# Low weight parts of 19 projection units per layer built by an adding transfer instead of a VectorE subtraction

## The chip, the core and the metric

The kernel runs on one core of a Trainium2 chip. The metric is the device time of one execution in microseconds (us); lower is better. A core has five engines that run their own instruction streams and meet only at semaphores: TensorE (PE, matrix products into PSUM), VectorE (DVE), ScalarE (ACT), GpSimd (POOL) and SyncE (SP), which here only issues transfers. POOL can issue transfers too.

## The reference

Two sequences of 256 tokens, width 1024, go through the same two layers. All numbers are fp32.

```python
def hybrid_layer(h, w_in, ..., ln2_g, ln2_b):
    proj = h @ w_in
    q, k, v, z, xbc, dt_raw = split(proj)
    q, k = rope(q), rope(k)
    attn_out = window_attention(q, k, v, attn_sink)      # 8 heads, 2 key heads, window 128
    xs, bm, cm = split(silu(depthwise_conv(xbc, 5 taps)))
    y = bidir_ssd(xs, dt_raw, ..., bm, cm) + ssd_d * xs  # 16 heads, two directions, chunks of 128
    ssd_out = rms_norm(y * silu(z), ssd_norm_g)
    mix = concatenate([attn_out, ssd_out]) @ w_out
    h = layer_norm(ALPHA * h + mix, ln1_g, ln1_b)
    gate, val = split(h @ w_up, 2)
    ffn = (silu(depthwise_conv(gate, 3 taps)) * val) @ w_down
    return layer_norm(ALPHA * h + ffn, ln2_g, ln2_b)
```

A layer norm stands in front of the first layer.

## The kernel before, in words

**Units.** All weights of a layer are cut into 105 units of 128 x 1024 fp32 (512 KB): unit 0 is the dt projection, 1 to 6 the keys, values and queries, 7 to 18 the channels of the convolution (`U_CONV` = 7), 19 to 26 the gate z (`U_Z` = 19), 27 to 38 the output projection (`U_OUT` = 27), 39 to 82 the up projection, 83 to 104 the down projection. Each lies in a slot of a ring of five (`RING` = 5, `AHEAD` = 4), in three tiles: `raw` as loaded by SP (line 477), `whi`, its value rounded to fp32r, and `wlo` = raw - whi. Activations are split in the same way (`hhi`, `hlo`), and each product of fp32 matrices is three products: hi x hi, lo x hi, hi x lo.

The three products in `three`:

```python
843    mm(out, whi[:, slot, cols], xhi, start=start, stop=False)
844    mm(out, whi[:, slot, cols], xlo, start=False, stop=False)
845    return mm(out, wlo[:, slot, cols], xhi, start=False, stop=stop)
```

**How a unit gets ready.** SP loads it once PE has used the unit five before it (`unit_used`). ACT copies it into `whi` (line 595) and raises `unit_hi`. DVE subtracts (line 1285) and raises `unit_split`, for which PE waits before it uses the unit. ACT and DVE do these at places of the schedule: step S (n) is both, SH (n) is ACT alone and SL (n) DVE alone.

**The order of work.** `mixer_schedule` writes a list of steps by hand, once; the programs of PE, ACT, DVE and POOL all walk through it and each does its own part of a step and skips the rest. The loop is over n = 0 to 26, a projection unit G (n) on PE in each round (24 products of 128 x 512), with other work between: in rounds 8 to 15 one pair i = n - 8 of the attention (a block of 128 queries with four heads): AS (scores, PE, line 1207), AM (mask and maximum, DVE), AX (exponentials, ACT), AD (denominators, DVE, line 1615), AN (scores times 1/denominator, POOL, line 556), and, a round later, AP (8 transposes on PE, line 1217: the first four wait for the first half of AN, the others for the second) and PT (ACT copies these to SBUF, line 782); AV (probabilities times values, PE, line 1227) comes after every second pair. ACT's part of a round of the attention is, in order, PT (i-1), AX (i), SH (n+4); POOL's is AN (i) and, from round 11 on, XS (line 564) and MV (line 575). Rounds 7 to 18 also carry the convolution: ACT centre tap (line 693), DVE four taps (line 1448), ACT tanh (SILU, line 728), DVE product (SIL2, line 1455), PE transposes T (line 1132), ACT evacuation (line 746).

From round 17 on come eight pairs of the state space part: SB and SF (PE, lines 1166 and 1177) give logarithms of decays in PSUM, SC (DVE, line 1559, two instructions) caps them, SE (ACT, lines 759 and 765) takes exponentials, SW (DVE, lines 1564 and 1568) adds and multiplies, SO (DVE, line 1574) multiplies the pair's `e_off`, SD (PE, line 1193, 32 small products) uses both, SY and SG (DVE) gather the result. After round 26 the output projection begins (GA, then G with `by_rows`, lines 980 to 982), while DVE and ACT finish the root mean square.

**The entry.** DVE normalises the four blocks of tokens (lines 1342 and 1345), PE transposes them (line 972 for the later ones), POOL makes `hlo` of the first sequence (line 531), then runs three memsets (lines 546 to 548) which the mixer's steps AA and SM need, then goes into the schedule. POOL's four loads of parameters (lines 542 and 543, two a layer) are the only transfers that it issues.

Of the kernel before, what the change touches and what calls it, by code (L numbers as in the profile page):

```python
# [19 lines left out]
ALU = mybir.AluOpType  # L20
ACT = mybir.ActivationFunctionType
# [4 lines left out]
DEPTH, D_MODEL, SEQ, NSEQ = 2, 1024, 256, 2  # L26
TOK = NSEQ * SEQ
BLK = 128
NBLK = TOK // BLK
# [5 lines left out]
CT = D_MODEL // P  # L35
# [9 lines left out]
U_CONV = 7  # L45
N_CONV = 12
U_Z = U_CONV + N_CONV
U_OUT = 27
N_OUT = 12
U_UP = U_OUT + N_OUT  # L50
U_DOWN = U_UP + 2 * FT
UNITS = U_DOWN + FT
RING = 5
AHEAD = RING - 1
LAST = 3
FINAL = 4
# [35 lines left out]
def mixer_schedule():  # L92
    steps = []
    for n in range(U_OUT):
        i = n - A0
        steps += [("G", n), ("E", n)]
        if U_Z <= n < U_OUT - 1:
            steps += [("SW", n - U_Z)]
# [4 lines left out]
        if i in (3, 5, 7):  # L103
            steps += [("AV", (i - 3) // 2)]
        if U_CONV < n < U_Z - 1:
            steps += [("SL", n - 1 + AHEAD)]
# [40 lines left out]
        if U_CONV <= n < U_Z:  # L147
            steps += [("SILU", n - U_CONV)]
            if not 0 <= i < 3:
                steps += [("SIL2", n - U_CONV)]  # L150
            if n == 17:
                steps += [("MV", 2), ("MV", 3)]
            if n - U_CONV >= 4:
                steps += [("XS", n - U_CONV)]
            if n == U_Z - 1:
                steps += [("SL", n - 1 + AHEAD)]
        if 15 <= n < 17:
            steps += [("MV", n - 15)]
        if n == 17:
            steps += [("SB", 0), ("SE", 0), ("SC", 0)]  # L160
        elif a >= 0:
            if a >= 1:
                steps += [("SD", a - 1)]
            if a < 7:
                steps += [("SB", a + 1), ("SE", 3 * a + 3)]
            if a == 0:
                steps += [("SC", 1), ("SE", 4), ("SO", 0)]
            elif a < 7:
                steps += [("SO", a), ("SC", a + 1), ("SE", 3 * a + 4)]
            else:  # L170
                steps += [("SW", 7), ("SO", 7)]
            steps += [("SL", n - 1 + AHEAD)]
            if a >= 1:
                steps += [("SY", a - 1)]
# [6 lines left out]
    steps += [("GA", (U_OUT, (2, 3))), ("GA", (U_OUT, (0, 1))), ("SD", 7), ("SY", 7), ("SG", 7), ("GA", (U_OUT, (4, 5)))]  # L181
    steps += [("RP", 1), ("RP", 3)] + [("SQ", c) for c in range(4, CT)] + [("RP", 5), ("RP", 7), ("SL", U_OUT - 1 + AHEAD)]
    steps += [("GA", (U_OUT + 1, range(6))), ("GA", (U_OUT + 2, range(6))), ("RS", 0)]
# [27 lines left out]
def trunk(nc, x_in, units, pm_d, pf_d, cn_d, gb_d, h_d, y_d):  # L211
    ctx = ExitStack()
    with ctx:
# [3 lines left out]
        def sem(name):  # L217
            return ctx.enter_context(nc.semaphore(name))
# [80 lines left out]
        def f(view):  # L299
            return view.bitcast(F32)  # L300
# [44 lines left out]
        h_spilled, h_loaded, gb_loaded, affined = sem("h_spilled"), sem("h_loaded"), sem("gb_loaded"), sem("affined")  # L345
        y_scaled, y_ready = sem("y_scaled"), sem("y_ready")

        h_low, h_lows, entry_low = sem("h_low"), sem("h_lows"), sem("entry_low")
# [68 lines left out]
        def unit(L, n):  # L417

            return L * UNITS + n

        def wait_high(eng, idx, s, j):
# [102 lines left out]
        def _(pool):  # L524
# [10 lines left out]
            for L in range(DEPTH):  # L535
# [8 lines left out]
                if L == 0:  # L544
                    lows(0)
                nc.gpsimd.memset(ln_dt[:, :, :, 1, :], 0.0).then_inc(ln_zeroed, 1)
                nc.gpsimd.memset(la_sides[:, 512:528], 0.0).then_inc(ln_zeroed, 1)
                nc.gpsimd.memset(f(off_w[:]), 0.0).then_inc(off_zeroed, 1)
                pool.wait_ge(pm_loaded, L * 16 + 16)
                for what, i in SCHED:  # L550
                    if what == "AN":

# [32 lines left out]
        def _(act):  # L585
            A = nc.scalar.activation

            def split(m):

                if m < DEPTH * UNITS:  # L590
                    act.wait_ge(raw_loaded[m % RING], (m // RING) * 16 + 16)
                    if m % UNITS == U_DT:
                        A(dt_part(whi, m, 0), dt_raw(m), ACT.Copy).then_inc(unit_hi, 1)
                    else:
                        A(whi[:, m % RING, :], raw[:, m % RING, :], ACT.Copy).then_inc(unit_hi, 1)  # L595

            def squares(idx, t):
# [240 lines left out]
        def _(pe):  # L838
# [92 lines left out]
            def first_units(idx, used):  # L931

                split_units = range(idx % 2 == 0, 2)
                pe.wait_ge(unit_split, used + 1)
                for j in range(2):
                    wait_low(pe, idx, 0, j)
                    for kind in ("hi hi", "hi lo"):
                        part(idx, used, 0, 0, kind, (2 * j, 2 * j + 1))
                pe.wait_ge(unit_split, used + 2)
                for kind in ("hi hi", "hi lo"):  # L940
# [11 lines left out]
                transposes(idx, 3)  # L952
                pe.wait_ge(unit_split, used + 3)
                for kind in ("hi hi", "hi lo", "lo hi"):
# [58 lines left out]
            def final_units(units4, used):  # L1013

                for t in range(NBLK):
                    for half in range(2):
                        for j, (slot, xhi, xlo) in enumerate(units4):
                            if t == 0 and half == 0:
                                pe.wait_ge(unit_split, used + j + 1)
                            last = three_rows(2 * t + half, slot, xhi, xlo, False, j == FINAL - 1)  # L1020
                        if half or t == NBLK - 1:
                            last.then_inc(acc_done, 1)
# [16 lines left out]
            for L in range(DEPTH):  # L1039
                for what, i in SCHED:  # L1040
# [7 lines left out]
                    elif what == "G" and i < U_OUT:  # L1048
# [7 lines left out]
                        elif i - 2 >= U_Z:  # L1056
                            pe.wait_ge(zs_done, L * CT + i - 2 - U_Z + 1)
                        pe.wait_ge(unit_split, L * UNITS + i + 1)
                        by_columns(unit(L, i) % RING, unit_bank(i))
                    elif what == "G":  # L1060
                        k = i - U_OUT
                        pe.wait_ge(unit_split, L * UNITS + i + 1)
                        before = None
# [9 lines left out]
                    elif what == "GT":  # L1073
                        pe.wait_ge(unit_split, unit(L, U_UP))
                        pe.wait_ge(sl_done, L * CT + CT)
                        last_units(2 * L + 1, [(unit(L, U_OUT + k) % RING, ahi[:, k, :], alo[:, k, :])
                                               for k in range(N_OUT - LAST, N_OUT)])
                    elif what == "GA":


                        u, banks = i
                        pe.wait_ge(unit_split, L * UNITS + u + 1)
                        if u == U_OUT and 2 in banks:
# [157 lines left out]
                for k in range(1, FT):  # L1241

                    if k >= 4:
                        pe.wait_ge(glu_done, L * FT + k - 3)
                    for half in range(1 if k == 1 else 0, 2):
                        n = U_UP + 2 * k + half
                        pe.wait_ge(unit_split, unit(L, n) + 1)
                        by_columns(unit(L, n) % RING, PAIR_BANK[k % 4] + half)

                count = LAST if L < DEPTH - 1 else FINAL  # L1250
                for k in range(FT - count):
                    pe.wait_ge(unit_split, unit(L, U_DOWN + k) + 1)
                    pe.wait_ge(glu_ready, L * FT + k + 1)
# [9 lines left out]
                if L < DEPTH - 1:  # L1263
                    pe.wait_ge(unit_split, unit(L, UNITS))
                pe.wait_ge(glu_ready, L * FT + FT)
# [8 lines left out]
        def _(dve):  # L1274
            V = nc.vector

            def split(m):

                if m < DEPTH * UNITS:
                    dve.wait_ge(unit_hi, m + 1)  # L1280
# [524 lines left out]
```

## Time and profile before

| | |
|---|---|
| median of 3 runs | 1307.52 us (1306.70 to 1307.57) |
| profiled execution | 1307.72 us |
| its span | 1305.9 us |
| PE busy | 1291.5 us (99%) |
| DVE busy | 823.5 us (63%) |
| ACT busy | 580.6 us (44%) |
| POOL busy | 96.6 us (7%) |
| granted clock of PE | 0.999 of full speed |

The span runs from the first to the last instruction; the rest of the execution's time lies around it. The ends of matmuls are modelled and overlap with the next, so a busy share of PE says little: one that waits shows as a gap before an instruction, with the releaser's name in brackets. Times of instructions below are us from the span's start.

### The profile page before, as it was taken

To read this page: it belongs to the slowest core of one execution; us is meant where nothing else is said; L and a number is where in the kernel's file an instruction comes from. 1 tells how busy PE (TensorE), PEld (TensorE's weight loads), DVE (VectorE), ACT (ScalarE), POOL (GpSimd) and SP (SyncE) were. 2 spreads that over 40 slices of the span, in tenths; PEclk is the share of its full clock that TensorE was granted. 3 is DMA by queue.
4 is the path that set the end of the run, shared out by engine and by line. 5 is a ranking of instruction groups with operands and counts; after the bars stand their busy time and mean duration, and the time that the engine had idled before them with its cause. 6 is when DMAs were issued, how large, how long until landed. Compare 5 with 4: busy or idle time off the path is not lost.

```text
span 1305.9 us, 16383 instructions
## 1 busy us (share of the span) xinstructions
PE 1291.5 (99%) x6688; PEld 1066.9 (82%) x6688; DVE 823.5 (63%) x1109; ACT 580.6 (44%) x875; POOL 96.6 (7%) x87
## 2 busy tenths in 40 slices
PE   9999999999999999999999999999999999999997
PEld 8877777889888888888898777778888888888886
DVE  7888799966444444342378987999654444443425
ACT  5766655436333333311276665544453333332112
POOL 2013400001000000000020234000000000000000
PEclk9999999999999999999999999999999999999999
DMA  5422212523333333333133212143233333333332
GB/s 188 163 68 56 65 59 65 182 62 126 96 97 98 96 99 95 128 98 97 55 129 135 65 50 81 52 143 113 82 98 97 98 97 97 97 97 128 98 97 112
DMA packets 33787, 129.24 MB, mean 99 GB/s; under 512 B 3793, under 2 KB 4209, under 8 KB 32561
## 3 DMA queue, kind: packets, MB, share of 16 engines
q1 hardware_dynamic: 33552, 127.91, 30.8%
q8 instruction: 53, 0.87, 0.3%
q0 software_dynamic: 160, 0.29, 0.1%
q14 instruction: 22, 0.17, 0.0%
HBM read 121.89 MB, written 6.29 MB: 98 GB/s over the span
## 4 chain that ended last, share of the span: by engine, by line
PE 90%; DVE 7%; issue 1%; ACT 1%; DMA 0%; DVEq 0%
PE ps L843 17%; PE ps L845 16%; PE ps L844 16%; PE ps L980 9%; PE ps L982 9%; PE ps L981 9%; PE ps L869 4%; PE ps L1193 1%; PE ps L1207 1%; PE ps L1217 1%; PE ps L1227 1%; DVE e_fwd L1559 1%; PE ps L972 1%; DVE e_fwd L1564 1%; DVE e_off L1574 1%
## 5 line engine op out<-in xcount | busy, mean ns | idle before, releaser
L843 PE MATMUL ps<-hhi,whi 128*128 128x512 f32 x1040 | 409.5, 394 | 0.0
L845 PE MATMUL ps<-hhi,wlo 128*128 128x512 f32 x1040 | 405.0, 389 | 0.0
L844 PE MATMUL ps<-hlo,whi 128*128 128x512 f32 x1040 | 404.8, 389 | 0.0
L1285 DVE TENSOR_TENSOR wlo<-raw,whi 128x1024 fp32r<-128x1024 f32 x208 | 253.9, 1222 | 150.3 <-ACT whi L595 150.3
L595 ACT ACTIVATE whi<-raw 128x1024 fp32r<-128x1024 f32 x208 | 219.3, 1056 | 218.0 <-DMA raw<-in_units 218.0
L843 PEld LDWEIGHTS ps<-hhi,whi 128*128 128x128 f32 x1040 | 195.2, 188 | 44.2 <-issue 4.9
L845 PEld LDWEIGHTS ps<-hhi,wlo 128*128 128x128 f32 x1040 | 195.2, 188 | 41.4
L844 PEld LDWEIGHTS ps<-hlo,whi 128*128 128x128 f32 x1040 | 195.3, 188 | 39.4
L980 PE MATMUL ps<-whi,uhi 128*128 128x512 f32 x352 | 137.1, 390 | 0.0
L982 PE MATMUL ps<-wlo,uhi 128*128 128x512 f32 x352 | 137.0, 389 | 0.0
L981 PE MATMUL ps<-whi,ulo 128*128 128x512 f32 x352 | 136.9, 389 | 0.0
L1660 DVE SCALAR_TENSOR_TENSOR gcv<-ps,pf,gcv 128x510 f32<-128x510 f32 x44 | 32.9, 748 | 157.2 <-ACT gcv L813 157.2
L813 ACT ACTIVATE gcv<-ps,pf 128x512 f32<-128x512 f32 x44 | 34.3, 780 | 168.9 <-PE ps L845 162.1
L1670 DVE TENSOR_TENSOR guf<-gsg,ps 128x512 f32<-128x512 f32 x44 | 30.2, 687 | 79.0 <-PE ps L845 78.4
L981 PEld LDWEIGHTS ps<-whi,ulo 128*128 128x128 f32 x352 | 66.1, 188 | 13.8
L982 PEld LDWEIGHTS ps<-wlo,uhi 128*128 128x128 f32 x352 | 66.1, 188 | 13.8
L980 PEld LDWEIGHTS ps<-whi,uhi 128*128 128x128 f32 x352 | 66.1, 188 | 13.5
L1448 DVE SCALAR_TENSOR_TENSOR cv<-ps,pm,cv 128x508 f32<-128x508 f32 (+1 forms) x96 | 71.4, 744 | 7.3 <-ACT cv L693 3.0
L980 PE MATMUL ps<-whi,ahi 128*128 128x512 f32 x192 | 75.8, 395 | 0.2
L981 PE MATMUL ps<-whi,alo 128*128 128x512 f32 x192 | 74.8, 389 | 0.0
L982 PE MATMUL ps<-wlo,ahi 128*128 128x512 f32 x192 | 74.8, 389 | 0.0
L531 POOL TENSOR_TENSOR hlo<-hfm,hhi 128x512 fp32r<-128x512 f32 x16 | 21.9, 1378 | 638.1 <-ACT hhi L630 637.8
(182 smaller groups left out, 1488.2 us busy)
## 6 DMA issues: line engine op xcount, KB each, us to landing
raw<-in_units SPq DMA_DIRECT2D x208, 512.0 KB, 3.7
gb<-in_gb SPq DMA_DIRECT2D x5, 1024.0 KB, 5.8
h_kept<-hb SPq DMA_DIRECT2D x2, 2048.0 KB, 9.2
ha<-h_kept SPq DMA_DIRECT2D x2, 2048.0 KB, 8.0
hb<-in_x SPq DMA_DIRECT2D x4, 512.0 KB, 5.9
out_y<-hb SPq DMA_DIRECT2D x8, 256.0 KB, 2.0
cn<-in_cn SPq DMA_DIRECT2D x1, 663.5 KB, 10.4
raw<-in_units SPq DMA_DIRECT2D x2, 128.0 KB, 3.5
```

The lines of the kernel that those rows point to most:

```text
L595: A(whi[:, m % RING, :], raw[:, m % RING, :], ACT.Copy).then_inc(unit_hi, 1)
L813: A(gcv[:], ps[:, bank, :], ACT.Identity, scale=pf[:, k * 3 + w0 + 1:k * 3 + w0 + 2], bias=pf[:, k + v0:k + v0 + 1]).then_inc(glu_center, 1)
L843: mm(out, whi[:, slot, cols], xhi, start=start, stop=False)
L844: mm(out, whi[:, slot, cols], xlo, start=False, stop=False)
L845: return mm(out, wlo[:, slot, cols], xhi, start=False, stop=stop)
L869: last = mm(out, w, x, start=c == 0 and kind == "hi hi", stop=stop, skip_group_check=True)
L980: mm(ps[:, bank, :], xhi[:, rows], whi[:, slot, cols], start=start, stop=False)
L981: mm(ps[:, bank, :], xlo[:, rows], whi[:, slot, cols], start=False, stop=False)
L982: return mm(ps[:, bank, :], xhi[:, rows], wlo[:, slot, cols], start=False, stop=stop)
L1285: V.tensor_tensor(wlo[:, m % RING, :], raw[:, m % RING, :], f(whi[:, m % RING, :]), ALU.subtract).then_inc(unit_split, 1)
L1448: V.scalar_tensor_tensor(out=dst[:, :, lo:hi], in0=src[:, :, lo + s:hi + s], scalar=pmc("conv_w", 5 * j + tap, 5 * j + tap + 1), in1=dst[: ...
L1660: V.scalar_tensor_tensor(out=dst[:, :, 1:SEQ], in0=src[:, :, 0:SEQ - 1], scalar=pf[:, k * 3 + w0:k * 3 + w0 + 1], in1=dst[:, :, 1:SEQ], op ...
```

## The change

For units 12 to 30 of each layer (`BY_DMA`) DVE no longer subtracts. ACT, after its copy into `whi`, writes -whi into `wlo`; POOL, at the step S or SH of the unit, waits for that and issues a transfer that adds the unit's weights from HBM onto `wlo`. PE waits for the transfer's semaphore (one per slot of the ring) instead of `unit_split`. In the schedule SL is placed anew (it does nothing for these units), SO (a) comes ahead of SC (a+1), and SW (7) at the head of round 26. In the first layer POOL's three memsets wait until DVE has normalised all four blocks.

```diff
+BY_DMA = range(12, 31)
...
-        if U_Z <= n < U_OUT - 1:
+        if n >= U_Z:
             steps += [("SW", n - U_Z)]
...
-        if U_CONV < n < U_Z - 1:
+        if U_CONV < n <= U_Z:
             steps += [("SL", n - 1 + AHEAD)]
...
-            if n == U_Z - 1:
-                steps += [("SL", n - 1 + AHEAD)]
...
                 steps += [("SB", a + 1), ("SE", 3 * a + 3)]
-            if a == 0:
-                steps += [("SC", 1), ("SE", 4), ("SO", 0)]
-            elif a < 7:
-                steps += [("SO", a), ("SC", a + 1), ("SE", 3 * a + 4)]
-            else:
-                steps += [("SW", 7), ("SO", 7)]
-            steps += [("SL", n - 1 + AHEAD)]
+            steps += [("SO", a)]
+            if a < 7:
+                steps += [("SC", a + 1), ("SE", 3 * a + 4)]
+            if n >= U_Z:
+                steps += [("SL", n + AHEAD)]
...
-    steps += [("RP", 1), ("RP", 3)] + [("SQ", c) for c in range(4, CT)] + [("RP", 5), ("RP", 7), ("SL", U_OUT - 1 + AHEAD)]
+    steps += [("RP", 1), ("RP", 3)] + [("SQ", c) for c in range(4, CT)] + [("RP", 5), ("RP", 7)]
...
+        low_minus = sem("low_minus")
+        low_added = [sem(f"low_added{k}") for k in range(RING)]
...
+        def by_dma(m):
+            return m < DEPTH * UNITS and m % UNITS in BY_DMA
+        def splits(m):
+            return sum(not by_dma(n) for n in range(m))
+        def adds(m):
+            return sum(by_dma(n) for n in range(m))
+        def wait_split(eng, m):
+            if by_dma(m):
+                eng.wait_ge(low_added[m % RING], 16 * sum(by_dma(n) and n % RING == m % RING for n in range(m + 1)))
+            else:
+                eng.wait_ge(unit_split, splits(m + 1))
...
                 if L == 0:
                     lows(0)
+                    pool.wait_ge(ln_normed, NBLK)
                 nc.gpsimd.memset(ln_dt[:, :, :, 1, :], 0.0).then_inc(ln_zeroed, 1)
...
                 for what, i in SCHED:
-                    if what == "AN":
+                    if what in ("S", "SH") and by_dma(unit(L, i)):
+                        m = unit(L, i)
+                        pool.wait_ge(low_minus, adds(m + 1))
+                        pool.dma_start(wlo[:, m % RING, :], units[m], accum_op=ALU.add).then_inc(low_added[m % RING], 16)
+                    elif what == "AN":
...
                         A(whi[:, m % RING, :], raw[:, m % RING, :], ACT.Copy).then_inc(unit_hi, 1)
+                    if by_dma(m):
+                        act.wait_ge(unit_hi, m + 1)
+                        A(wlo[:, m % RING, :], f(whi[:, m % RING, :]), ACT.Copy, scale=-1.0).then_inc(low_minus, 1)
...
-                        pe.wait_ge(unit_split, L * UNITS + i + 1)
+                        wait_split(pe, unit(L, i))
...
             def split(m):
-                if m < DEPTH * UNITS:
+                if m < DEPTH * UNITS and not by_dma(m):
                     dve.wait_ge(unit_hi, m + 1)
```

All of PE's waits for `unit_split` are replaced as the one shown.

## Rows read from the trace of the kernel before

**Rows 1.** The page, part 1: busy us, share, instructions of each engine.

```profile
PE 1291.5 (99%) x6688; PEld 1066.9 (82%) x6688; DVE 823.5 (63%) x1109; ACT 580.6 (44%) x875; POOL 96.6 (7%) x87
```

**Rows 2.** Waits of PE: who waited for whom, us in total, times, longest.

```profile
PE ps L1193 <- DVE e_off L1574: 4.3, 4, 1.4
...
PE ps L972 <- DVE hb L1345: 0.8, 1, 0.8
```

**Rows 3.** The page, part 5: groups by line; busy us, mean ns, idle before.

```profile
L1285 DVE TENSOR_TENSOR wlo<-raw,whi 128x1024 fp32r<-128x1024 f32 x208 | 253.9, 1222 | 150.3 <-ACT whi L595 150.3
L595 ACT ACTIVATE whi<-raw 128x1024 fp32r<-128x1024 f32 x208 | 219.3, 1056 | 218.0 <-DMA raw<-in_units 218.0
```

**Rows 4.** Timeline, first state space pair: start us, us, instruction, [idle before, releaser].

```profile
168.52 1.22 DVE L1574 TENSOR_TENSOR e_off<-e_off,cb 128x1024 f32<-128x1024 f32 x1
170.00 0.33 PE L1193 MATMUL ps<-e_fwd,xs_tm 128*64 128x128 f32 x2 [1.43 <-DVE e_off L1574]
```

**Rows 5.** Timeline of the entry, DVE and POOL.

```profile
16.15 2.76 DVE L1345 TENSOR_SCALAR hb<-hb,st 128x1024 f32<-128x1024 f32 x1
17.41 0.95 POOL L548 MEMSET off_w<- 128x1024 f32 x1
```

**Rows 6.** Timeline, ACT and POOL at a layer norm.

```profile
657.30 0.62 ACT L630 ACTIVATE hhi<-hfm 128x512 fp32r<-128x512 f32 x1
658.00 1.29 POOL L531 TENSOR_TENSOR hlo<-hfm,hhi 128x512 fp32r<-128x512 f32 x1 [351.02 <-ACT hhi L630]
```

**Rows 7.** The page, part 6: transfers; KB each, median us to landing.

```profile
raw<-in_units SPq DMA_DIRECT2D x208, 512.0 KB, 3.7
```

**Rows 8.** Timeline, attention pair 0: ACT's copy, POOL's AN, PE's transposes.

```profile
73.99 1.07 ACT L595 ACTIVATE whi<-raw 128x1024 fp32r<-128x1024 f32 x1
74.67 2.04 POOL L556 TENSOR_TENSOR sc<-sc,ast 128x512 f32<-128x512 f32 x2 [56.31 <-DVE ast L1615]
76.11 1.31 PE L1217 MATMUL ps<-cn,sc 128*128 128x128 f32 x8
```

**Rows 9.** Timeline, transposes of pairs 1 to 3, ACT between the last two.

```profile
83.89 1.09 PE L1217 MATMUL ps<-cn,sc 128*128 128x128 f32 x8
...
93.34 1.09 PE L1217 MATMUL ps<-cn,sc 128*128 128x128 f32 x8
...
94.47 1.03 ACT L782 ACTIVATE p_t<-ps 128x1024 f32<-128x1024 f32 x1 [0.41 <-PE ps L1217]
...
97.29 1.07 ACT L595 ACTIVATE whi<-raw 128x1024 fp32r<-128x1024 f32 x1
...
100.90 1.09 PE L1217 MATMUL ps<-cn,sc 128*128 128x128 f32 x8
```

**Rows 10.** Timeline of POOL at the second layer's start: loads of 80 and 60 KB.

```profile
670.48 0.58 POOL L542 DMA_DIRECT2D pm<-in_pm  x1 [0.56 <-POOL hlo L531]
671.06 0.53 POOL L543 DMA_DIRECT2D pf<-in_pf  x1
671.59 0.33 POOL L546 MEMSET ln_dt<- 128x256 f32 x1
```

**Rows 11.** Timeline, attention pair 5: POOL's AN, PE's transposes.

```profile
116.21 2.04 POOL L556 TENSOR_TENSOR sc<-sc,ast 128x512 f32<-128x512 f32 x2 [5.76 <-DVE ast L1615]
...
120.53 1.09 PE L1217 MATMUL ps<-cn,sc 128*128 128x128 f32 x8
```

**Rows 12.** Timeline, attention pair 7: ACT's copy, PE's transposes.

```profile
135.22 1.08 ACT L595 ACTIVATE whi<-raw 128x1024 fp32r<-128x1024 f32 x1
...
139.00 1.03 PE L1217 MATMUL ps<-cn,sc 128*128 128x128 f32 x8
```

**Rows 13.** Timeline, round 18: ACT's copy of unit 22, tanh, PE's T.

```profile
156.54 1.05 ACT L595 ACTIVATE whi<-raw 128x1024 fp32r<-128x1024 f32 x1
...
159.94 0.63 ACT L728 ACTIVATE xsc<-cv 128x512 f32<-128x512 f32 x1
...
161.35 0.33 PE L1132 MATMUL ps<-cn,xsc 128*128 128x128 f32 x1 [0.18 <-DVE xsc L1455]
```

More of the change, by code:

```diff
@@ L933, in first_units @@
                 split_units = range(idx % 2 == 0, 2)
-                pe.wait_ge(unit_split, used + 1)
+                wait_split(pe, used)
                 for j in range(2):
@@ L938, in first_units @@
                         part(idx, used, 0, 0, kind, (2 * j, 2 * j + 1))
-                pe.wait_ge(unit_split, used + 2)
+                wait_split(pe, used + 1)
                 for kind in ("hi hi", "hi lo"):
@@ L952, in first_units @@
                 transposes(idx, 3)
-                pe.wait_ge(unit_split, used + 3)
+                wait_split(pe, used + 2)
                 for kind in ("hi hi", "hi lo", "lo hi"):
@@ L1018, in final_units @@
                             if t == 0 and half == 0:
-                                pe.wait_ge(unit_split, used + j + 1)
+                                wait_split(pe, used + j)
                             last = three_rows(2 * t + half, slot, xhi, xlo, False, j == FINAL - 1)
@@ L1061, in _ @@
                         k = i - U_OUT
-                        pe.wait_ge(unit_split, L * UNITS + i + 1)
+                        wait_split(pe, unit(L, i))
                         before = None
@@ L1073, in _ @@
                     elif what == "GT":
-                        pe.wait_ge(unit_split, unit(L, U_UP))
+                        wait_split(pe, unit(L, U_UP) - 1)
                         pe.wait_ge(sl_done, L * CT + CT)
@@ L1081, in _ @@
                         u, banks = i
-                        pe.wait_ge(unit_split, L * UNITS + u + 1)
+                        wait_split(pe, unit(L, u))
                         if u == U_OUT and 2 in banks:
@@ L1246, in _ @@
                         n = U_UP + 2 * k + half
-                        pe.wait_ge(unit_split, unit(L, n) + 1)
+                        wait_split(pe, unit(L, n))
                         by_columns(unit(L, n) % RING, PAIR_BANK[k % 4] + half)
@@ L1251, in _ @@
                 for k in range(FT - count):
-                    pe.wait_ge(unit_split, unit(L, U_DOWN + k) + 1)
+                    wait_split(pe, unit(L, U_DOWN + k))
                     pe.wait_ge(glu_ready, L * FT + k + 1)
@@ L1263, in _ @@
                 if L < DEPTH - 1:
-                    pe.wait_ge(unit_split, unit(L, UNITS))
+                    wait_split(pe, unit(L, UNITS) - 1)
                 pe.wait_ge(glu_ready, L * FT + FT)
```

## The prediction

> **What bounds the kernel now.** I read the page's busy times first [rows 1]: TensorE (PE) is busy for 99% of the span, and no other engine for more than 63%. A busy PE isn't proof, since the ends of matmuls are modelled, so the second view was who PE waited for [rows 2]: at its head stand 4.3 us for VectorE (DVE) in the state space stage; what follows is short, 0.8 us of it for DVE at the entry. So PE's own stream of matmuls bounds the kernel. A change off PE can win back about 5 us at most, and whatever it makes PE wait for is lost for good, because PE has no slack in which to catch up. That turns the question round: not how much work leaves DVE, but what comes late for PE.
>
> **What the change takes away.** For the 19 units 12 to 30 of a layer (19 x 2 = 38) the subtraction in line 1285 goes from DVE, 1.22 us each [rows 3], some 23 us a layer. Nearly all of this is free time already. Two places gain.
> (a) The state space stage: PE waits for the `e_off` products before SD, 4.3 us in four waits [rows 2]. The product SO(0) starts at 168.52 [rows 4], behind the two cappings of SC(1), each as wide as a split (128x1024); the change puts SO(0) ahead of both, by two such operations, some 2.3 us earlier. That is more than the 1.43 us which PE waited there [rows 4]. SC(1), for whose first capping PE's SF(1) waits, gets SO's time ahead of it and loses that of the dropped split of unit 22: it starts when it did. SW(7), now ahead of the last gate product, changes places with an operation that PE doesn't wait for. The other wait of a layer is at SD(7), for SO(7); there eight splits of 1.22 us are gone from DVE by then. I take all 4.3 us as gained. Late next would be PE's own order, so no new wait.
> (b) The entry: the fourth normalisation took 2.76 us beside GpSimd (POOL), whose last memset ends at 18.36 inside it [rows 5]; PE waits 0.8 us for it [rows 2]. The memsets now wait for it. Gain 0.8 us. Their later place costs nothing: the first reader (AA) comes five units later; without that cover PE would wait for 1 us of memset.
> Sum of the gains: 5.1 us.
>
> **What it adds.** Each of the 38 units gets three things.
> 1. A second copy on ScalarE (ACT), whi negated into wlo, like line 595: 1.06 us [rows 3], behind a wait for the first copy. From ACT's end to a waiting POOL there pass 0.08 us (657.92 to 658.00) [rows 6]; I take 0.08 for both hand-overs.
> 2. On POOL, at the same place of the schedule (S or SH), a wait for that copy and the issue of an adding transfer.
> 3. 512 KB more of traffic. A plain load of that size lands in 3.7 us [rows 7]. The split of unit 12 is copied from 73.99 on [rows 8] and read by PE after 94.43, when the transposes of pair 2 are over [rows 9]: 17 us for the transfer. The other units have about as much. I cost it at nothing; without that cover it would be PE's wait, a rival below.
> The semaphore functions only rename what PE waits for. "Narrower waits of score banks" has no counterpart in the diff, and I give it nothing.
>
> **What stands behind the new wait.** In the schedule SH(n+4) is ahead of AN(n-8), the normalising of the attention scores on POOL, and PE's transposes AP wait for these. Before, POOL skipped SH; AN had only to wait for DVE's denominators. Now AN starts at the earliest at (end of the first copy) + 0.08 + 1.06 + 0.08 + d = + 1.22 + d, where d is what the issue costs POOL. The trace shows no adding transfer. Nearest rows: two loads of 80 and 60 KB over the same 128 partitions were issued back to back in 0.58 and 0.53 us, and a memset ran at once behind them, long before they landed [rows 10]. So d = 0.6 us. From below the bound is 0 (it can't be negative: the wait itself is in the 1.22). From above: if the 0.05 us by which 80 KB is dearer than 60 KB scales with bytes, 512 KB costs 0.58 + 432 x 0.0025 = 1.7 us. I take 0.6, because number of rows and engine are the same; the ends go into the range.
>
> With 1.82 us:
> - **Pair 0.** The copy ends at 75.06, AN starts at 76.88 instead of 74.67 [rows 8]: 2.21 us later. Before, the transposes ended 0.71 us after AN did (77.42, 76.71); they had no slack. PE loses 2.21.
> - **Pairs 1 and 3.** Here a loop closes. From the end of the transposes of one pair: 0.04 to ACT's evacuation (94.43 to 94.47), 3.89 to the end of the hi copy behind the exponentials (98.36), 1.82, AN 2.04 [rows 8], and 0.71 as above: 8.50 us. PE's period between the ends was 7.56 (77.42 to 84.98 and 94.43 to 101.99) [rows 8, 9]. PE loses 0.94 twice. Pair 2 has a period of 9.45 and loses nothing. In pairs 4 to 6 other work stands between; in the tightest, pair 5, PE began 2.28 us after AN had ended (118.25 to 120.53) [rows 11], as long as AN comes later: nothing, but no more to spare.
> - **Pair 7.** The copy ends at 136.30, AN starts at 138.12 and ends at 140.16, the transposes at 140.87 instead of 140.03 [rows 12]: 0.84.
> - **Unit 22.** On ACT the copy at 156.54 is followed without a gap by three others and, at 159.94, by the tanh of the last convolution, for which DVE's product and then PE's transposes (161.35, already waiting) are due [rows 13]. 1.06 + 0.08 more on ACT delays them by 1.1.
> Elsewhere ACT is idle before what PE needs next of it, and this idle time hides the second copy; where it didn't, a unit would cost up to 1.1 us, as unit 22 does.
> Loss per layer 2.21 + 2 x 0.94 + 0.84 + 1.1 = 6.0 us; the second layer has the same pattern (the four waits of [rows 2] are two a layer), so 12.1. Net 12.1 - 5.1 = +7.0 us. The profiled execution took 1307.7 us (span 1305.9 and 1.8 around it), 0.2 above the median of 1307.5, so nothing is scaled: **1314.5 us**.
>
> **Where a rule differs.** The rows say that an issue holds POOL for 0.53 us or more [rows 10]. The Trainium skill, page "DMA: Bandwidth & Descriptors", section "Anatomy of one DMA", puts the dispatch at about 50 ns and the generation of descriptors at "small, variable". By it d would be near zero. That is the rival "free issue". The row decides until an adding transfer is seen.
>
> **The rivals.**
> - **Free issue (not slower).** POOL hands the transfer over and goes on at once: d = 0. Pair 0 still loses 1.61 (wait and copy), pairs 1 and 3 0.34 each, pair 7 0.24, unit 22 1.1: 3.6 a layer, net 7.3 - 5.1 = +2.2, 1309.7 us. The point of decision is d = 0.05 us: above it the time leaves the 0.2% band. For it: only the small size of d in the rows. Against: three rows back to back.
> - **Gains alone (faster).** AN isn't held, because POOL's queue or the transposes have slack that I misread; only unit 22 loses. 2.2 - 5.1 = -2.9, 1304.6 us. For it: pair 5 does have slack [rows 11]. Against: pair 0 had none.
> - **Long issue.** d = 1.7, since an adding transfer is more work to describe, or its description is held by DVE. The loop is 9.60: pair 0 loses 3.31, pairs 1 and 3 2.04 each, pair 2 0.15, pair 7 1.94, unit 22 1.1, 10.6 a layer, net +16.1, 1323.6 us. For it: DVE and POOL do hold each other up, as the entry shows (2.76 us) [rows 5]. Against: by the code DVE's work at those moments, the taps of the convolution, reads PSUM and not two tiles of SBUF.
> - **Slow transfer.** Adding is read, read and write. If it took 10 us and they were served one by one, while PE takes a unit in 7.56 to 9.45 us [rows 9], 8.5 in the mean, then 19 x 1.5 us less the 17 us of lead are lost: some 11 a layer on top, 1337 us. Against: a plain load takes 3.7 us [rows 7].
>
> **How the numbers follow.** Forecast 0.62, free issue 0.10, gains alone 0.10, long issue 0.13, slow transfer 0.05. About 0.2% (2.6 us) is what a measurement of this kernel can tell from no change: faster 0.10; same 0.12 (free issue, and the low edge of the forecast); slower 0.78. The range goes from 1309 (d = 0) to 1323 (d = 1.7) and leaves out the slow transfer and the gains alone.
>
> **What would show it.** After the change AN(0) should start near 76.1 (76.88 less the 0.8 of the entry), 1.8 us behind the end of its copy; PE's list of waits should have L1217 on POOL's line 556 at its head, some 10 us in all, four times or so a layer in the attention stage and none there in pairs 4 to 6; L1132 on DVE 1455 should rise to about 2.6; the waits on L1574 and on L1345 should be gone. POOL's rows give d directly. Wrong would be: AN starting at DVE's denominator as before, transposes without waits, a wait of PE's for a landing transfer, or waits on L1574 that stay.

## The result, and the profile after

The changed kernel takes **1329.55 us** (median of 6, 1329.06 to 1329.98) against 1307.12 us before (median of 6, 1306.63 to 1307.57) on the same chip. Single executions of the kernel before lie near 1306.6 or near 1307.6 us, so a difference of 1 us between two medians is read here from the traces beside it. The ratio is 1.0171, 95% interval [1.0161, 1.0182]. The forecast was 1314.5 us, in a range of 1309 to 1323: slower was right, the size was a third of what was measured (+7 against +22), and the time lies outside the range.

The page's busy times after, against [rows 1]:

```profile
PE 1296.4 (98%) x6688; PEld 1067.6 (80%) x6688; DVE 810.2 (61%) x1071; ACT 620.5 (47%) x913; POOL 126.9 (10%) x125
```

PE does the same 6688 matmuls, 5 us longer in busy time, in a span that is 22 us longer (1328.1 us): it waits. Whom for says the view of PE's waits (us in total, times, longest), against [rows 2]:

```profile
PE ps L1243 <- POOL sc L579: 8.8, 9, 2.6
PE ps L1158 <- DVE alo L1644: 5.5, 4, 1.7
PE ps L1158 <- DVE xsc L1481: 5.4, 4, 1.6
...
PE ps L1203 <- DVE e_fwd L1585: 1.1, 2, 0.6
PE ps L1192 <- issue: 1.0, 2, 0.5
```

L1243 are the transposes AP, L1158 the transposes T, L1203 is SF, L1192 SB. The waits for `e_off` are gone, as forecast, and the one for POOL stands at the head, as forecast. The second row was in no forecast: T waits for `alo`, which DVE makes, and DVE has less work than before.

PE runs the same matmuls in the same order in both kernels, so I read how late each one starts after the change, less how late it started before, and where this lateness grows. (A gap of PE, below, is the distance from one matmul's start to the next, less the usual one, 0.23 us for 512 columns.) In us a layer:

| place | forecast to add | added, layer 1 | added, layer 2 |
|---|---|---|---|
| AP, pairs 0, 1, 3, 7 | 4.9 | 6.3 | 5.2, and 2.1 at half clock, see below |
| T(6) and T(8) | 0 | 3.1 | 3.1 |
| T(10) and SF(0) behind it | 0 | 2.3 | 2.3 |
| T(11) | 1.1 | 0.9 | 0.95 |
| SB(2) | 0 | 0.6 | 0.6 |
| SD(0) and SD(7) | -2.15 | -2.3 | -2.3 |

With 0.1 at T(5) and T(9) and still less elsewhere, PE falls behind by 11.1 us in layer 1 and 12.2 in layer 2; less 1.05 at the entry that is the whole difference of the two spans, 22.2 us. Ahead of the first normalised block PE waits longer than before (1.4 us for 0.6 in this view), but only because its first matmuls ran faster; the wait ends at 8.54 us for 8.55 and adds nothing.

**What POOL does.** Transfer rows of the page (KB and us to landing), against [rows 7]:

```profile
raw<-in_units SPq DMA_DIRECT2D x208, 512.0 KB, 3.6
wlo<-in_units POOLq DMA_DIRECT2D x38, 512.0 KB, 5.6
```

Timeline of the first pair, ACT, POOL and PE, against [rows 8]:

```profile
72.94 1.07 ACT L618 ACTIVATE whi<-raw 128x1024 fp32r<-128x1024 f32 x1
74.04 1.06 ACT L621 ACTIVATE wlo<-whi 128x1024 fp32r<-128x1024 f32 x1
...
75.66 0.92 POOL L573 DMA_DIRECT2D wlo<-in_units  x1 [56.65 <-ACT wlo L621]
76.28 2.36 POOL L579 TENSOR_TENSOR sc<-sc,ast 128x512 f32<-128x512 f32 x2
...
77.71 0.66 PE L1243 MATMUL ps<-cn,sc 128*128 128x128 f32 x4 [2.58 <-POOL sc L579]
78.70 0.55 PE L1243 MATMUL ps<-cn,sc 128*128 128x128 f32 x3 [0.34 <-POOL sc L579]
```

Transfers land in 5.6 us (5.3 to 7.7) and PE waits for none of them. AN starts 0.62 us after the issue does: d = 0.6, as taken. But the issue begins 0.56 us behind the copy's end (0.30 in the later rounds, 0.55 again in round 8 of layer 2) where I took 0.08, AN takes 2.36 us for its two products instead of 2.04, and PE waits ahead of the transposes of the second half too.

**The part that was missed**, DVE and POOL. First round 11 of the kernel before, then rounds 11 and 12 of the changed one:

```profile
98.35 2.04 POOL L556 TENSOR_TENSOR sc<-sc,ast 128x512 f32<-128x512 f32 x2 [5.99 <-DVE ast L1615]
...
100.40 0.69 DVE L1455 SCALAR_TENSOR_TENSOR xsc<-xsc,cv 128x512 f32<-128x512 f32 x1 [0.69 <-ACT xsc L728]
```

```profile
103.13 0.88 POOL L573 DMA_DIRECT2D wlo<-in_units  x1 [6.50 <-ACT wlo L621]
103.73 2.35 POOL L579 TENSOR_TENSOR sc<-sc,ast 128x512 f32<-128x512 f32 x2
...
103.38 3.25 DVE L1481 SCALAR_TENSOR_TENSOR xsc<-xsc,cv 128x512 f32<-128x512 f32 x1 [0.75 <-ACT xsc L754]
...
114.23 2.77 DVE L1481 SCALAR_TENSOR_TENSOR xsc<-xsc,cv 128x512 f32<-128x512 f32 x1 [0.57 <-ACT xsc L754]
...
119.38 0.68 DVE L1644 TENSOR_TENSOR alo<-ps,ahi 128x512 fp32r<-128x512 f32 x1
...
120.21 0.63 PE L1158 MATMUL ps<-cn,xsc 128*128 128x128 f32 x4 [1.68 <-DVE alo L1644]
```

L1481 is SIL2, DVE's last step of a convolution, `xsc` times `cv`, both in SBUF. Before, AN was over 0.01 us ahead of it, in all of rounds 11 to 15. Now AN is under way while SIL2 runs, and SIL2 takes 3.25 us in round 11 instead of 0.69; it ends 0.55 us after AN's end (106.08, 106.63). In rounds 12 to 15 it takes 2.76 to 2.77. DVE is late with all that follows: from SIL2 of round 12 (over at 117.00) it works nearly without a break up to `alo`, and PE's T(6) at 120.21 waits for that. The same happens beside MV, POOL's decay products of round 17:

```profile
159.90 4.06 POOL L598 TENSOR_TENSOR heads<-cum_a,cn 128x1024 fp32r<-128x1024 f32 x2
...
161.52 3.00 DVE L1481 SCALAR_TENSOR_TENSOR xsc<-xsc,cv 128x512 f32<-128x512 f32 x1 [0.70 <-ACT xsc L754]
...
164.58 0.66 PE L1158 MATMUL ps<-cn,xsc 128*128 128x128 f32 x4 [1.57 <-DVE xsc L1481]
```

The 16 products of this kind took 11.1 us before and 37.4 after. The Trainium skill, page "SBUF — State Buffer", section "Who interferes with whom", says that a DVE instruction with two SBUF inputs contends with a GpSimd instruction that reads SBUF, and that whoever issues first blocks the other fully. That the two contend the traces bear out. That the first one wins they do not, by the starts that the profile shows: in rounds 12 to 15 SIL2 started 0.14 us behind AN, in round 11 it started 0.35 us ahead of it, and it was the one held in either case. The experiments show more of it.

**Layer 2** differs in one place. Windows of PE behind the wait for pair 0 (window, length, PE busy and matmuls, granted clock, DMA share, GB/s):

```profile
730.00:732.50 2.50, 0.05 (x1) 0.88 0.88 223
732.50:734.50 2.00, 2.00 (x9) 0.50 0.92 160
734.50:738.70 4.20, 4.20 (x12) 0.50 0.17 33
738.70:742.00 3.30, 3.30 (x17) 1.00 0.23 21
```

After 2.5 us with next to no work TensorE was granted half its clock, 1.2 GHz instead of 2.4, for 6 us; matmuls came every 0.43 us instead of 0.23. That cost about 2.4 us and hid pair 1's 1.4 behind it, so 1.0 is left as the difference to layer 1. There the same wait (2.58 us in the timeline above, 2.53 here) was followed by no such stretch.

### The profile page after: what moved, and what is told of

Same layout as the page of the kernel before. It is cut to its first block, busy times and chain, and to the rows that moved or that the text cites. A ratio compares the mean times of both kernels' runs of the same rounds, so it can differ in the third digit from the quotient of the medians.

```text
span 1328.1 us, 16421 instructions
## 1 busy us (share of the span) xinstructions
PE 1296.4 (98%) x6688; PEld 1067.6 (80%) x6688; DVE 810.2 (61%) x1071; ACT 620.5 (47%) x913; POOL 126.9 (10%) x125
## 4 chain that ended last, share of the span: by engine, by line
PE 87%; DVE 5%; ACT 5%; POOL 1%; issue 1%; DMA 0%; SPq 0%; DVEq 0%; ACTq 0%; POOLq 0%
PE ps L869 16%; PE ps L870 16%; PE ps L871 16%; PE ps L1006 9%; PE ps L1007 9%; PE ps L1008 9%; PE ps L895 5%; PE ps L1219 2%; DVE xsc L1481 2%; ACT sc L799 2%; ACT whi L618 1%; DVE ast L1630 1%; PE ps L998 1%; POOL sc L579 1%; ACT wlo L621 1%
## 5 line engine op out<-in xcount | busy, mean ns | idle before, releaser
L1311 DVE TENSOR_TENSOR wlo<-raw,whi 128x1024 fp32r<-128x1024 f32 x170 | 207.8, 1224 | 149.4 <-ACT whi L618 149.4
```

The source lines that it names most:

```text
L1311: V.tensor_tensor(wlo[:, m % RING, :], raw[:, m % RING, :], f(whi[:, m % RING, :]), ALU.subtract).then_inc(unit_split, 1)
```

## The experiments

Times are medians; "before" ran beside each group at 1307.6 to 1307.7 us.

**1. AN first.** Two theories were left: POOL's order (and DVE's product behind it), or transfers and copies as such. In rounds 8 to 15 the issue goes behind AN:

```diff
 for what, i in SCHED:
+    if held and before_was_an:
+        add(held.pop())
+    before_was_an = what == "AN"
     if what in ("S", "SH") and by_dma(unit(L, i)):
-        m = unit(L, i)
-        pool.wait_ge(low_minus, adds(m + 1))
-        pool.dma_start(wlo[:, m % RING, :], units[m], accum_op=ALU.add).then_inc(low_added[m % RING], 16)
+        if i - AHEAD < A0 + 8:
+            held.append(unit(L, i))
+        else:
+            add(unit(L, i))
```

(`add` holds the three lines taken out.)

> The changed kernel with one thing moved: in rounds 8 to 15 POOL issues the round's added transfer behind its two normalising products of the scores (AN) instead of ahead of them. Transfers, ACT's second copies and DVE's relief stay. Theory (POOL's order, and behind it DVE's two-input product SIL2, which stood at 2.76 to 3.25 us instead of 0.69 wherever AN came late and fell on it): AN is back at its old place, PE's waits for sc go from 8.8 us to under 1.5, SIL2 is back at 0.69 in rounds 12 to 15, PE's waits for alo and xsc (5.5 and 5.4) keep at most the 1.3 a layer ahead of T(11) and what MV does to T(10) (up to 1.7 a layer); 1329.6 - 8 - 6 to 9 - 4 (the low clock of layer 2, which followed on a wait of 2.7) = 1305 to 1312. Rival (the transfers themselves or ACT's copies cost the time, wherever POOL issues): the waits for alo and xsc stay, 1318 or more.

**1309.64 us**, ratio 1.0018 [1.0009, 1.0028]: 20 us of the 22 hang on the place of 16 issues and of the waits ahead of them. Round 12 here:

```profile
104.94 2.04 POOL L590 TENSOR_TENSOR sc<-sc,ast 128x512 f32<-128x512 f32 x2 [4.28 <-DVE ast L1652]
106.92 0.87 POOL L574 DMA_DIRECT2D wlo<-in_units  x1
...
107.53 0.69 DVE L1492 SCALAR_TENSOR_TENSOR xsc<-xsc,cv 128x512 f32<-128x512 f32 x1 [0.57 <-ACT xsc L765]
```

No wait for `sc` or `alo` is left, no half clock either, and SIL2 beside an issue alone is as fast as ever. Round 17, whose issue was not moved, keeps its 2.99 us.

**2. The wait without the transfer.** `pool.dma_start(...)` is taken out, the wait for `low_minus` stays, and PE waits for the same copy; the low parts of these units lack the weights themselves.

> Left out: the added transfers. POOL still waits for ACT's second copy at the same place, PE waits for that copy instead of the transfer, and the low parts of units 12 to 30 lack the weights themselves. It tells the wait for ACT's copy from the issue and the transfer. Theory (AN is late by whichever is longer, the copy plus 0.6 us of issue): without the issue AN comes 0.6 to 0.9 us earlier than in the changed kernel, so PE's wait ahead of pair 0 falls from 2.7 to about 1.9 and those of pairs 1 and 3 from 0.95 to under 0.3, and SIL2 stays stretched only where AN still reaches into it (rounds 12, 13): about 1314 to 1321. Rival (all of it is the issue or the transfer: port, queue or HBM traffic): 1302 to 1308. Rival (all of it is the wait for the copy): 1327 to 1330.

**1314.08 us**, ratio 1.0052 [1.0037, 1.0067]. So the wait for ACT's copy costs some 4.5 us more than AN first (the transposes of pairs 0, 1, 3 and 7 are later by 1.6, 0.3, 0.7 and 0.7 a layer, while T(10) loses 1.1 less than in run 1), and the issue with its transfer 15.5 on top. SIL2 was at 0.89 us in the mean, 1.12 in round 11.

**3. The rest alone.** `BY_DMA = ()`.

> The rest of the change alone: no unit's low part is made by a transfer, DVE subtracts all of them; SO ahead of SC, the new places of SL and SW, and the later memsets stay. Theory of the prediction (the gain in the state space stage comes from DVE's relief of the subtractions, 4.3 us; the memsets give 0.8 to 1.0): 1306 to 1307. Rival (the reordering alone gives the 4.3 us): 1302 to 1303. Rival (SO ahead of SC costs where DVE still subtracts): over 1308.

**1307.73 us**, ratio 1.0003 [0.9994, 1.0013]. Neither: the wait for `e_off` is gone, and in its place stand 1.2 us before SB(2), 0.5 before SF(1), 0.35 more before T(11) and 0.6 at the first output unit (GA). The timeline shows why:

```profile
169.71 0.58 ACT L743 ACTIVATE zt<-ps 128x512 f32<-128x512 f32 x1
170.19 1.02 ACT L791 ACTIVATE e_off<-ps 128x1024 f32<-128x1024 f32 x1
...
171.30 0.51 PE L1192 MATMUL ps<-heads,own_w 32*128 32x512 f32 x4 [1.03 <-issue]
```

SB(2) waits for pair 1's three exponentials, and ACT ends the last of them at 171.21; it is late because they stand behind DVE's cappings SC(1), which now stand behind SO(0). The order moved a wait and did not remove it: from T(11) to GA the stage gained 2.1 us a layer at SD and lost 2.6 in these four places, and the microsecond of the entry covers that.

**4. Only the late units.** `BY_DMA = range(23, 31)`.

> Added transfers only for units 23 to 30 of each layer, which POOL issues in rounds 19 to 26, when it has no other work; units 12 to 22 are subtracted by DVE as before. Theory (all the loss comes from the issues and copies of rounds 8 to 18, all the gain of the 4.3 us from DVE's relief in rounds 19 to 26, plus 1.0 at the entry): 1301.5 to 1303.5, below both kernels. Rival (the second copies on ACT or the issues cost in the state space stage too): 1305 or more.

**1306.11 us**, ratio 0.9991 [0.9982, 1.0000]. DVE's relief in rounds 19 to 26 is worth 1.6 us against run 3 (the gap of 0.6 a layer at GA is gone), not the 4.3 expected; SB(2) keeps its 1.2.

**5. All issues at the round's end.** As 1, with every issue up to round 25 at the head of the next round (`if held and what in ("G", "GA")`), so behind MV too.

> As the run with AN first, but POOL issues every round's added transfer only as the next round begins, behind its other work of the round too (the decay products MV, line 598 of the changed kernel, and XS). With AN first 4.4 us a layer of PE's gaps were left: 1.73 before T(10) and 0.73 behind it, where DVE's SIL2 stood at 2.99 us against MV, then 1.29 and 0.65 in rounds 18 to 20. Theory (MV, issued at 150.25 us, is late by the wait for ACT's copy and the issue; in time it would be done by about 152.3, when SIL2 comes): SIL2 there is under 1.3 us, the first two gaps fall to under 0.7 together, 1309.6 - 3 to 4.5 = 1305 to 1307. Rival (MV is where DVE's relief has brought SIL2 forward into it, the issue is innocent): 1309 to 1310.

**1305.03 us**, ratio 0.9981 [0.9972, 0.9991]. SIL2 is at 0.69 us in all 16 cases and T(10) waits no more.

**6. ACT's copy alone.** As 3, but ACT makes the high copy of units 12 to 30 twice and only then signals it.

> ACT's part alone: as the run with no added transfers (1307.7 us; DVE subtracts everything, POOL issues nothing), but for units 12 to 30 ACT makes the high copy twice, so that it is busy as long as with the negated copy, and DVE's subtraction waits for the second. Theory of the prediction (the copy costs only where it stands ahead of the last tanh, unit 22: T(11) 1.1 us later in each layer): 1309 to 1311. Rival (ACT's copies cost nothing to speak of, PE's wait ahead of T(11) is DVE's): 1307.5 to 1308.3. Rival (they delay the exponentials of attention and of the state space stage as well): over 1312.

**1308.89 us**, 1.2 above run 3; T(11)'s gap goes from 0.70 to 1.28 in each layer, all else stays. The step on unit 22 had the right mechanism and half the size against run 3, which already had 0.35 more there than the kernel before.

**7. AN late in the kernel before**, with no transfer anywhere:

```diff
 pool.wait_ge(as_den, L * 8 + i + 1)
+for k in range(3):
+    nc.gpsimd.memset(pad[:, k], 0.0)
```

> The kernel before, with AN alone made late: in rounds 8 to 15 POOL does three small memsets of a spare tile (together about 0.5 us) between its wait for the divisors and AN. No transfer, no second copy, no new wait. Theory (DVE's product of two SBUF tiles, SIL2, is held while AN runs and for 0.56 us after its end): in rounds 12 to 15, where SIL2 starts within 0.1 us of AN's old end, it goes from 0.69 to 1.0 to 1.2 us; PE waits about 0.5 us ahead of pair 0 and little elsewhere; 1308 to 1310. Rival (the stretched SIL2 of the changed kernel is due to the transfer's reads and writes, not to AN): SIL2 stays at 0.69 in all 16 cases.

**1308.39 us**, ratio 1.0006 [0.9997, 1.0015]. The memsets made AN 0.34 us late, not 0.5:

```profile
98.91 2.04 POOL L559 TENSOR_TENSOR sc<-sc,ast 128x512 f32<-128x512 f32 x2
...
100.64 0.85 DVE L1458 SCALAR_TENSOR_TENSOR xsc<-xsc,cv 128x512 f32<-128x512 f32 x1 [0.70 <-ACT xsc L731]
```

AN ends at 100.95, SIL2 at 101.49, 0.54 later: held to the end, by AN alone. So it was in all of rounds 11 to 15 of both layers, each time 0.85 us, a smaller stretch than the 1.0 to 1.2 expected, in the right places.

**8. Pair 0 alone.** As 1, for round 8 only (`i - AHEAD == A0`).

> The changed kernel with the issue put behind AN in round 8 alone (pair 0 of either layer); all other rounds as changed. Theory (the fall of the granted clock to about 0.5 for 6 us in layer 2 followed on PE's wait of 2.7 us there, and cost 4.4 us, behind which AN's wait of pair 1 was hidden): no stretch at half clock, PE's two waits of 2.7 and the slower first matmuls behind them (0.5 each) gone, pair 1 of layer 2 waits as in layer 1 (1.5): 1329.6 - 6.4 - 4.4 + 1.5 = 1320 to 1321.5. Rival (the low clock is not tied to that wait): it shows elsewhere, 1324 or more.

**1326.60 us**: missed by 5 to 6. Pair 0's gaps went, but what pair 1 adds grew from 1.4 to 2.3 us, and the half clock was not gone, it had moved to layer 1, behind that wait:

```profile
85.80:87.20 1.40, 1.06 (x8) 0.69 1.01 173
87.20:89.80 2.60, 2.60 (x8) 0.51 0.48 93
89.80:92.00 2.20, 2.20 (x11) 1.00 0.00 0
```

In layer 2 the same wait (1.71 us, 1.72 in layer 1) had no such stretch.

**9. The issue's time without an issue.** As 2, with five memsets of a spare tile behind the wait in rounds 8 to 17.

> Left out: the added transfers, as in the run with the wait alone (1314.1 us), so the low parts of units 12 to 30 lack the weights. In place of the issue POOL does, in rounds 8 to 17, five small memsets of a spare tile behind its wait for ACT's copy, about the 0.6 us that an issue holds it. It tells POOL's time at the head of AN and MV from what the transfer itself does (its traffic, its descriptions). Theory (it is the time alone; the 0.6 us bring AN's start behind DVE's reach for SIL2): SIL2 at 2.7 to 3.3 us in rounds 11 to 15, PE's waits for sc near 8 and for alo near 5; 1324 to 1330. Rival (the transfer itself slows AN and SIL2): 1314 to 1318, SIL2 under 1.5 us in the mean.

**1317.61 us**: the theory, that POOL's time alone does it, fell. The memsets held POOL for only 0.4 us where an issue holds it 0.6, but AN did overlap SIL2 as in the changed kernel, here in round 12:

```profile
110.32 2.49 POOL L584 TENSOR_TENSOR sc<-sc,ast 128x512 f32<-128x512 f32 x2
...
110.92 0.99 DVE L1486 SCALAR_TENSOR_TENSOR xsc<-xsc,cv 128x512 f32<-128x512 f32 x1 [0.58 <-ACT xsc L759]
```

SIL2 came in between AN's two products (it ended at 111.91, 0.55 after the first one's end at 111.36), and AN's second product waited, 1.49 us instead of 1.04.

**10. A small load in place of the transfer.** As 2, with a plain load of 128 rows of 64 bytes behind the wait.

> Left out: the added transfers (the low parts of units 12 to 30 lack the weights). In their place POOL issues, at the same points and behind the same wait, a plain load of 128 rows of 64 bytes into a spare tile. The pads of 0.43 us in place of the issue gave 1317.6 us only, and there SIL2 came in between AN's two products (1.48 us instead of 3.25 in round 11). So an issue does more than take time. Theory (the issue itself: behind one, DVE's product isn't let in between POOL's operations, whatever the bytes): SIL2 at 2.7 to 3.3 us in rounds 11 to 15, AN at 2.3 to 2.4 for two, PE's waits for alo near 5; 1325 to 1330. Rival (the 512 KB on their way, read or written beside AN): SIL2 under 1.5 us, 1315 to 1319.

**1325.20 us**, ratio 1.0137 [1.0121, 1.0152]. The issue does it, with no bytes to speak of, again in round 12:

```profile
112.92 0.57 POOL L576 DMA_DIRECT2D pad<-in_pm  x1 [5.74 <-ACT wlo L624]
113.52 2.04 POOL L582 TENSOR_TENSOR sc<-sc,ast 128x512 f32<-128x512 f32 x2
...
113.66 2.46 DVE L1484 SCALAR_TENSOR_TENSOR xsc<-xsc,cv 128x512 f32<-128x512 f32 x1 [0.57 <-ACT xsc L757]
```

SIL2 came 0.14 us after AN had begun and was held through both products. In round 11 of run 9 it had come 0.10 us after AN's start, as early as here, and was let in between them (1.48 us), which speaks against the 0.2 us by which the memsets were shorter than an issue. The losses at T(6) and T(8), 1.6 and 0.95 us a layer, are here and not in run 9.

**11. A plain load of the same 512 KB**, `accum_op` left away.

> POOL issues a plain load of the unit's 512 KB onto the low part at the same points, not an adding one, so the low parts of units 12 to 30 hold the whole weights. All waits as changed. Theory (any issue does it): as the changed kernel, 1327 to 1330, SIL2 at 2.7 to 3.3 us. Rival (only the adding transfer does): SIL2 under 1.5 us, 1315 to 1320.

**1325.11 us**, ratio 1.0137 [1.0120, 1.0153]. As run 10, and below the 1327 to 1330 expected: the size costs nothing, and the adding costs the last 4.4 us. The adding transfer's issue is shown busy for 0.88 us, a plain one's for 0.58, though AN starts 0.60 us after it in either case; AN takes 2.36 us behind the adding one and 2.04 behind the plain one, and what waits for AN (transposes, SIL2, T(6), T(8), T(10)) is later by about these 0.3 us each time.

**12. Unit 22's copy late.** As 5, with ACT's second copies of units 22 and 23 in round 19 ahead of pair 1's exponentials, and POOL's issues at the same place.

> As the run with the issues at the round's end (1305.0 us), with one thing more: ACT's second copies of units 22 and 23, and POOL's issues of them, come in round 19 ahead of the exponentials of pair 1, not in rounds 18 and 19 right behind the first copies. Theory (the copy of unit 22, ahead of the last tanh, makes SIL2, T(11) and what DVE has behind it 1.0 us late: PE gaps of 1.28 and 0.65 us a layer): T(11)'s gap falls to 0.2 to 0.4, that before SB(2) to under 0.3; 1305.0 - 2 x 1.3 = 1302 to 1303. Rival (T(11)'s wait is DVE's taps, not the copy): 1304.5 to 1305.5.

**1303.04 us**, ratio 0.9965 [0.9952, 0.9979]. T(11)'s gap is 0.31 us; SB(2) kept its wait (0.6 more than before) against the expectation, so that wait does not come from unit 22's copy.

**13. A version with the gains and not the losses.**

```diff
-BY_DMA = range(12, 31)
+BY_DMA = range(21, 31)
...
+if n == 17:
+    steps += [("LM", 21)]
...
+if a == 0:
+    steps += [("LM", 22), ("LM", 23)]
...
+if a == 0:
+    steps += [("SC", 1), ("SE", 4), ("SO", 0)]
```

LM is ACT's second copy and POOL's issue. LM(21) stands behind MV and XS, LM(22) and LM(23) ahead of SB(1) and SE(3) in round 19, the others behind SH as in the change.

> A version meant to keep the gains and drop the losses: added transfers for units 21 to 30 only (DVE subtracts the others), the second copies of 21, 22 and 23 and their issues placed where ACT and POOL stand idle (behind MV and XS in round 17, and in round 19 ahead of pair 1's exponentials), and in round 19 SC(1) ahead of SO(0) as in the kernel before. Theory (the order alone only moved the wait of pair 0's product to SB and SF; what shortens the stage is one subtraction less ahead of SC(1)): of the 1.59 and 0.89 us of PE's gaps before SD(0) and SD(7) a layer nothing over 0.3 is left, and the entry's 1.0 stays gone: 1307.6 - 1.0 - 2 x 2.5 = 1301 to 1303. Rival (the wait for e_off comes back as the order does): 1304 to 1306.

**1302.29 us**, ratio 0.9959 [0.9946, 0.9971], the fastest of all. PE's gaps before SB, SD and SF are gone (0.26 before SD is the largest); T(11) keeps 0.31. Beside run 12, which has the copies of 22 and 23 at the same place and no subtraction of 22 either, this one has SC(1) ahead of SO(0), and SB(2) doesn't wait.

**14. The entry alone**: in the kernel before, `pool.wait_ge(ln_normed, NBLK)` ahead of the three memsets.

> The kernel before with the later entry memsets alone (POOL waits for the four normalisations before its three memsets). Theory: the fourth normalisation takes 1.57 us instead of 2.76 and PE's transposes come 1.0 us earlier; 1306.3 to 1306.9. Rival (the start of the kernel is bound by its loads, and the gap only moves): 1307.3 to 1307.8.

**1306.62 us**, ratio 0.9993 [0.9984, 1.0001]: medians 1.0 apart, and PE's matmuls behind the fourth block start 1.0 us earlier in the trace. The fourth normalisation takes 1.58 us there, and 1.57 in the changed kernel, against 2.76 in [rows 5].

## Why the prediction failed, step by step

- **"That turns the question round: not how much work leaves DVE, but what comes late for PE."** Right, but I followed lateness along POOL to PE only, and not from POOL across to DVE.
- **The step that failed** stands in the rival "Long issue": "Against: by the code DVE's work at those moments, the taps of the convolution, reads PSUM and not two tiles of SBUF". The taps do. SIL2, right behind them, doesn't, and it began 0.01 us after AN's end, so what a late AN does to DVE went into the sum at nothing. A related hold-up stood in a row, the fourth normalisation beside a memset (2.76 us, and 1.58 without it in run 14) [rows 5]; there DVE reads one tile of SBUF and the memset none, and I used the row only to reckon the entry. T(6), T(8), T(10) and SF(0) cost 2 x 5.4 us for it, seven tenths of the 15 us by which the forecast was short. "Elsewhere ACT is idle before what PE needs next of it" was beside the point.
- **AN behind the wait.** The mechanism, the pairs (0, 1, 3 and 7, none in 4 to 6) and d = 0.6 were right. The rule of the rival "free issue" did not hold here: an issue held POOL 0.60 us. Mis-sized were the hand-over from ACT to an issue, 0.30 to 0.56 us for 0.08, and AN's own time, 2.36 for 2.04. In layer 1 the pairs added 3.0, 1.4, 1.5 and 0.4 for 2.21, 0.94, 0.94 and 0.84, with T(5) and T(9) behind them 1.5 us a layer more.
- **Unit 22.** T(11) came 0.95 us later, for 1.1 forecast; run 12 shows that it is this copy.
- **The gains.** The entry: 1.0 for 0.8. The state space stage: 2.3 us a layer were won at SD, for 2.15, and SC(1) did start when it did (5.46 us after SIL2's start for 5.65). Wrong was "Late next would be PE's own order, so no new wait": before, pair 1's exponentials ended 9.75 us after T(11) had begun, and PE, which began SB(2) 10.55 after it, would have been there at 9.1 without the 1.46 of SD(0). The long wait had hidden a shorter one, 0.6 us. The runs have all four combinations, by what then waits in layer 1: unit 22's subtraction with SC(1) first, SD(0) (before); with SO(0) first, SB(2) for 1.1 and SF(1) (runs 3 and 4); no subtraction with SO(0) first, SB(2) for 0.6 (the changed kernel, runs 5 and 12); no subtraction with SC(1) first, none (run 13). It takes both, the dropped subtraction and the old order, and run 13 wins what the prediction had put down as the gain, 5.3 us for 5.1.
- **Slow transfer**: 5.6 us to land and no wait, as said.
- **The half clock** was in no step. Its net share is small, 1.0 us between the layers.

Sum over the forecast of +7: 10.9 (SIL2 beside AN and MV), 3.0 (AN), 1.2 (SB), 1.0 (clock), less 0.3 (T(11)), 0.3 (SD) and 0.2 (entry) make the +22 that was measured.

Of the signs that the prediction named, AN(0) at 76.28 us (76.1 was said), the waits for POOL at the head (8.8 us for some 10) and the end of the waits for `e_off` came true. T's waits for SIL2 stand at 5.4 us where 2.6 was said: that was the sign of the missing term.

## What to carry to other kernels

When a step is moved on one engine, look at what runs on its neighbour at its new time, and not only at who waits for it: here a product of two SBUF tiles stood 0.01 us behind POOL's work, and that was no slack at all. Put the issue of a transfer behind an engine's urgent work, not ahead of it; its landing had microseconds to spare. And a long wait can hide a shorter one behind it: ask when the next thing would be ready if PE came earlier.

## What the hardware showed that I had not expected

- A two-input DVE product that meets POOL's products is held to the end of the one in flight and ends 0.55 us after it (runs 2, 7 and 9); a POOL product that then waits for it takes 1.49 us instead of 1.04. If POOL has issued a transfer just ahead of its two products, the DVE product is held to the end of both (2.46 us for 64-byte rows, 2.77 for the adding one), whether it starts 0.14 us behind the first of them or 0.35 ahead. Why an issue has this effect is open.
- POOL's products directly behind an adding issue are shown 0.3 us longer each (1.35 for 1.04 us) without being spaced wider; behind a plain one they aren't.
- A wait for ACT is passed on to a compute instruction of POOL in 0.06 to 0.17 us, to an issue in 0.30 and, after 47 to 57 us of idling, in 0.54 to 0.57.
- Behind its longest waits ahead of AP, 1.7 to 2.6 us, TensorE was granted half its clock for some 2 to 6 us in five of eight cases (layer 2 of the changed kernel, layer 1 of runs 8 and 11, both layers of run 10), and full clock in the other three. The waits of the same 1.7 us ahead of T(6) in the changed kernel and run 8 were never followed by such a stretch. The Trainium skill, page "TensorE: Matmul & The Clock Gate", section "Part 1: The HAM clock gate (the "warmup" mystery)", has the gate watch activity in its own time, which no kernel sets; by that the same wait may be caught or not, as it was here.
